# A two-layer hybrid trunk in float32: layer 0's shift and scale computed ahead, the gate's third behind the context's attention

## The reference

```
mod_x = silu(c)     @ w_ada[l] + b_ada[l]       # 3072 columns: shift, scale, gate
mod_c = silu(c_ctx) @ w_ada[l] + b_ada[l]
shift, scale, gate = split(mod, 3)
h = rmsnorm(x, g_pre) * (1 + scale) + shift     # the same for the context
p = h @ w_in                                    # projections of attention, conv, retention, fourier
y = merge(window_attention, short_conv, bidirectional_retention, fourier)
x = x + gate * rmsnorm(y, g_post)
```

## Time and profile before

| | us |
|---|---|
| three runs | 2643.99 to 2648.36, median 2647.52 |
| profiled execution | 2651.15 |
| its span | 2649.1 |
| TensorE busy | 2506.8 (95%) |
| VectorE, ScalarE, GpSimd busy | 1145.0, 1110.8, 1217.4 |
| chain that ended last | TensorE 79%, issue 8%, GpSimd 6%, VectorE 5%, ScalarE 2% |
| load of one unit (256 KB, 512-byte rows), issue to landing | 2.9 |
| load of `r_table` (320 KB), issue to landing | 2.9 |
| load of one `w_ada` block (1536 KB) | 9.1 |

### The profile page before, as it was taken

One profiled execution on the slowest core, in us unless ns is written; L12 is line 12 of the kernel. 1 busy time (PEld: TensorE's weight loads), 2 busy tenths in 40 slices (PEclk: granted clock), 3 DMA queues, 4 the chain that ended last, 5 costly groups with the idle time before them and its releaser, 6 DMA issues.

```text
span 2649.1 us, 39623 instructions
## 1 busy us (share of the span) xinstructions
PE 2506.8 (95%) x12993; PEld 2099.8 (79%) x12993; DVE 1145.0 (43%) x1698; ACT 1110.8 (42%) x2319; POOL 1217.4 (46%) x992
## 2 busy tenths in 40 slices
PE   7888979999999999999999979999999999999997
PEld 1887877899888767787888867898888788888886
DVE  2443655388153433334243367483444433333332
ACT  2635543288221454434433343594214433343332
POOL 1566963223222368865555442122212555555553
PEclk9898989999999999999999989999999999999999
DMA  6345663100121155544433431001210333344333
GB/s 238 96 126 163 175 186 105 45 4 6 48 65 33 36 148 159 159 127 131 147 109 107 146 116 40 24 2 34 64 43 21 106 111 111 111 135 143 111 111 119
DMA packets 390040, 262.37 MB, mean 99 GB/s; under 512 B 16006, under 2 KB 361238, under 8 KB 388378
## 3 DMA queue, kind: packets, MB, share of 16 engines
q1 hardware_dynamic: 377248, 227.07, 29.0%
q10 hardware_dynamic: 12668, 33.67, 3.6%
HBM read 251.23 MB, written 9.45 MB: 98 GB/s over the span
## 4 chain that ended last, share of the span: by engine, by line
PE 79%; issue 8%; POOL 6%; DVE 5%; ACT 2%; DMA 0%; ACTq 0%; POOLq 0%; DVEq 0%; SPq 0%
PE ps L671 75%; POOL w_lo L572 5%; PE ps L830 2%; DVE r_prev L2012 1%; DVE softmax_stats L1905 1%; DVE x_post L2227 0%; DVE a_probT_lo L1646 0%; DMA w_ada<-in_w_ada 0%; ACT a_prob L1334 0%; PE ps L770 0%; DVE norm_tmp L1791 0%; DVE a_out_sum L1646 0%; PE ps L816 0%; DVE proj_raw L1646 0%; PE ps L703 0%
## 5 line engine op out<-in xcount | busy, mean ns | idle before, releaser
L572 POOL TENSOR_TENSOR w_lo<-w_raw,w_hi 128x512 fp32r<-128x512 f32 x818 | 1113.5, 1373 | 1101.4 <-ACT w_hi L1166 1094.1
L671 PE MATMUL ps<-hT_hi,w_hi 128*128 128x512 f32 (+1 forms) x2528 | 948.7, 375 | 47.5 <-POOL w_lo L572 29.6
L671 PE MATMUL ps<-hT_lo,w_hi 128*128 128x512 f32 (+1 forms) x2528 | 934.8, 370 | 0.0
L671 PE MATMUL ps<-hT_hi,w_lo 128*128 128x512 f32 (+1 forms) x2528 | 934.5, 370 | 0.0
L1166 ACT ACTIVATE w_hi<-w_raw 128x512 fp32r<-128x512 f32 x818 | 507.5, 629 | 1006.9 <-PE ps L671 855.6
L671 PEld LDWEIGHTS ps<-hT_hi,w_hi 128*128 128x128 f32 x2528 | 484.4, 192 | 143.2 <-POOL w_lo L572 30.0
L671 PEld LDWEIGHTS ps<-hT_hi,w_lo 128*128 128x128 f32 x2528 | 484.3, 192 | 79.2
L671 PEld LDWEIGHTS ps<-hT_lo,w_hi 128*128 128x128 f32 x2528 | 484.9, 192 | 75.6
L1646 DVE TENSOR_TENSOR merge_tmp<-merge_tmp,ps 128x512 f32<-128x512 f32 (+1 forms) x160 | 101.6, 635 | 674.0 <-PE ps L671 411.4
L1646 DVE TENSOR_TENSOR merge_tmp<-merge_tmp 128x512 f32<-128x512 f32 (+1 forms) x120 | 170.8, 1423 | 4.1
L671 PE MATMUL ps<-yT_hi,w_hi 128*128 128x512 f32 (+1 forms) x400 | 148.3, 371 | 10.6 <-POOL w_lo L572 5.4
(11 more groups left out here) (260 smaller groups left out, 2800.0 us busy)
## 6 DMA issues: line engine op xcount, KB each, us to landing
w_raw<-in_w_in SPq DMA_DIRECT2D x512, 256.0 KB, 2.9
w_raw<-in_w_o_rest SPq DMA_DIRECT2D x120, 256.0 KB, 2.8
w_raw<-in_w_out SPq DMA_DIRECT2D x80, 256.0 KB, 2.6
w_ada<-in_w_ada SPq DMA_DIRECT2D x8, 1536.0 KB, 9.1
w_raw<-in_w_ada SPq DMA_DIRECT2D x48, 256.0 KB, 2.7
w_raw<-in_w_o_attn SPq DMA_DIRECT2D x40, 256.0 KB, 2.7
x_tile_first<-in_x ACTq DMA_DIRECT2D x8, 512.0 KB, 7.0
w_raw<-in_dft_x SPq DMA_DIRECT2D x16, 256.0 KB, 2.7
```

Of the source, the lines that this page charges most:

```text
L572: eng.tensor_tensor(w_lo[:, r, :], raw[:, r, :], w_hi[:, r, :].bitcast(F32), ALU.subtract).then_inc(sem["w_split"], tally.up("w_split"))
L671: return eng.matmul(dst, lhsT, rhs, start=start, stop=stop)
```

## The change

It has three parts. The context's tokens are loaded in `constants`, ahead of mask and `small`, and squared and scaled before the modulation. The modulation computes only shift and scale (2048 of 3072 columns): each block of `w_ada` is copied to a high part on ScalarE, its low part made on VectorE, and TensorE multiplies both with four columns, the high and low parts of the two silu vectors (64 fp32r products). The gate's third is loaded by ScalarE behind the context's attention, ahead of `r_table`, and multiplied in float32 in three groups between the projections; VectorE makes the gate row at that stage's end. The steps of `log_gamma` move to that stage too.

```diff
-        w_ada = at("w_ada", [P, KT, 3 * D], 0)
+        w_ada = at("w_ada", [P, KT, 2 * D], 0)
+        w_ada_lo = at("w_ada_lo", [P, KT, 2 * D], 0, F32R)
+        w_ada_hi = at("w_ada_hi", [P, 3, 2 * D], W + 2304, F32R)
+        w_ada_gate = [at("w_ada_gate", [P, KT - 1, D], Z + 3072), at("w_ada_gate_last", [P, D], W + 8448)]
...
             def ada(layer, k):
-                if k > 1:
-                    eng.wait_ge(ada_in[k - 2], 16)
-                eng.dma_start(w_ada[:, k, :], a["w_ada"][layer][k * P:(k + 1) * P, :]).then_inc(ada_in[k], 16)
+                if k > 2:
+                    eng.wait_ge(ada_in[k - 3], 16)
+                eng.dma_start(w_ada[:, k, :], a["w_ada"][layer][k * P:(k + 1) * P, 0:2 * D]).then_inc(ada_in[k], 16)
...
-            def modulation(l):
-                eng.wait_ge(sem["silu_c"], tally.take("silu_c"))
+            def modulation():
+
                 for k in range(KT):
-                    eng.wait_ge(ada_in[k], 16)
-                    for n in range(6):
-                        ins = mm(ps[0:2, n, :], sT[:, :, k], w_ada[:, k, n * 512:(n + 1) * 512], k == 0, k == KT - 1)
+                    eng.wait_ge(sem["ada_low"], tally.take("ada_low"))
+                    for n in range(4):
+                        c = slice(n * 512, (n + 1) * 512)
+                        mm(ps[0:4, n, :], s4[:, k, :], w_ada_hi[:, k % 3, c], k == 0, False)
+                        ins = mm(ps[0:4, n, :], s4[:, k, :], w_ada_lo[:, k, c], False, k == KT - 1)
...
+            def gate_sums(first, last):
+
+                eng.wait_ge(sem["gate_in"], tally.now("gate_in", 16 * 4))
+                for k in range(first, last):
+                    for n in range(2):
+                        c = slice(n * 512, (n + 1) * 512)
+                        w = w_ada_gate[0][:, k, c] if k < KT - 1 else w_ada_gate[1][:, c]
+                        ins = mm(ps[0:2, 6 + n, :], sT[:, :, k], w, k == 0, k == KT - 1)
+                        if k == KT - 1:
+                            ins.then_inc(sem["gate_sums"], tally.up("gate_sums"))
...
-                project(p, 8)
+                if p.opens:
+                    project(p, 4)
+                    gate_sums(0, 2)
+                    project(p, 2)
+                    gate_sums(2, 5)
+                    project(p, 2)
+                    gate_sums(5, KT)
+                else:
+                    project(p, 8)
...
                 eng.dma_start(ident[:, :], a["ident"]).then_inc(sem["const_in"], tally.up("const_in", 16))
+                tokens(passes[0], 0)
                 eng.dma_start(m_mask[:, :, :], a["mask"]).then_inc(sem["const_in"], tally.up("const_in", 16))
...
+                squares(p, 0)
+                for k in range(KT):
+                    eng.wait_ge(ada_in[k], 16)
+                    if k > 2:
+                        eng.wait_ge(sem["ada_used"], tally.take("ada_used"))
+                    act(w_ada_hi[:, k % 3, :], w_ada[:, k, :]).then_inc(sem["ada_high"], tally.up("ada_high"))
...
+            def gate_thirds(p):
+
+                l = p.layer
+                w = a["w_ada"][l][:, 2 * D:3 * D].rearrange("(k p) n -> p k n", p=P)
+                eng.dma_start(w_ada_gate[0][:, :, :], w[:, 0:KT - 1, :]).then_inc(sem["gate_in"], tally.up("gate_in", 16))
+                eng.dma_start(w_ada_gate[1][:, :], w[:, KT - 1, :]).then_inc(sem["gate_in"], tally.up("gate_in", 16))
...
                 stage_end(eng, tally, "act")
+                if p.opens:
+                    gate_thirds(p)
                 eng.dma_start(r_tab[:, :, :], a["ret"]).then_inc(sem["ret_in"], tally.up("ret_in", 16))
-                tile_range(p, B_U, B_B)
+                for t in range(B_U, B_B):
+                    tile_range(p, t, t + 1)
+                    if p.opens:
+                        log_gamma(t - B_U)
+                if p.opens:
+                    log_gamma(2)
                 decay_tables()
                 tile_range(p, B_B, R_Q)
+                if p.opens:
+                    gate_row(p)
                 stage_end(eng, tally, "act")
...
                 scaled(p, 0)
+                for k in range(KT):
+                    eng.wait_ge(sem["ada_high"], tally.take("ada_high"))
+                    tt(w_ada_lo[:, k, :], w_ada[:, k, :], w_ada_hi[:, k % 3, :].bitcast(F32), ALU.subtract).then_inc(
+                        sem["ada_low"], tally.up("ada_low"))
...
+            def gate_row():
+
+                eng.wait_ge(sem["gate_in"], 16 * 4)
+                for n in range(2):
+                    eng.wait_ge(sem["gate_sums"], tally.take("gate_sums"))
+                    c = slice(n * 512, (n + 1) * 512)
+                    tt(m_bias[0:2, c], ps[0:2, 6 + n, :], m_bias[0:2, c], ALU.add).then_inc(sem["dve_own"], tally.up("dve_own"))
+                eng.wait_ge(sem["dve_own"], tally.now("dve_own"))
+                tt(m_gate[0:2, :], m_bias[0:2, :], m_gate[0:2, :]).then_inc(sem["gate_made"], tally.up("gate_made"))
```

More of the change, by code:

```diff
@@ L233, in trunk @@
         x_tile = at("x_tile", [P, 4, D], W + 10240)
-        m_mask = at("mask_f32", [P, 2, P], W + 10240)
+        m_mask = at("mask_f32", [P, 2, P], W + 16384)
         n_sq = at("norm_square", [P, 4, 512], W + 14336)
@@ L1103, in _ @@
                 if p.ctx:
-                    modulation(p.layer)
+                    modulation()
                 elif p.kept:
@@ L1216, in modulation @@
-                tokens(p, 0)
-                squares(p, 0)
+                eng.dma_start(m_biasT[:, :], a["b_ada_cols"][l]).then_inc(sem["small_in"], tally.up("small_in", 16))
+                squares(p, 0)
[4 more added lines that the diff above has]
+                    act(w_ada_hi[:, k % 3, :], w_ada[:, k, :]).then_inc(sem["ada_high"], tally.up("ada_high"))
@@ L1218, in modulation, with gate_row @@
+            def gate_row(p):
                 eng.wait_ge(sem["gate_made"], tally.take("gate_made"))
-                eng.dma_start(gate_rows[l], m_gate[0:2, :]).then_inc(sem["gate_out"], tally.up("gate_out", 16))
-                eng.wait_ge(sem["gate_out"], tally.now("gate_out"))
+                eng.dma_start(gate_rows[p.layer], m_gate[0:2, :]).then_inc(sem["gate_out"], tally.up("gate_out", 16))
             def tokens(p, b):
@@ L1716, in modulation @@
                     tt(s4[:, :, 2 + s], sT[:, s, :], s4[:, :, s].bitcast(F32), ALU.subtract).then_inc(sem["dve_own"], tally.up("dve_own"))
-                eng.wait_ge(sem["small_in"], tally.take("small_in", 16 * 6))
-                for step in range(4):
-                    log_gamma(step)
+                eng.wait_ge(sem["dve_own"], tally.now("dve_own"))
                 scaled(p, 0)
-                for n in range(6):
-                    eng.wait_ge(sem["mod_rows"], tally.take("mod_rows"))
-                    c = slice(n * 512, (n + 1) * 512)
-                    tt(m_rows[0:2, c], ps[0:2, n, :], m_bias[0:2, c], ALU.add).then_inc(sem["mod_saved"], tally.up("mod_saved"))
@@ new lines, in modulation @@
+                for n in (1, 3):
+                    eng.wait_ge(sem["mod_rows"], n + 1)
+                    eng.tensor_copy(m_rows[0:4, n * 512:(n + 1) * 512], ps[0:4, n, :]).then_inc(sem["mod_saved"], tally.up("mod_saved"))
+                tally.skip("mod_rows", 4)
+                eng.wait_ge(sem["small_in"], tally.take("small_in", 16 * 5))
+                eng.wait_ge(sem["mod_cols"], tally.take("mod_cols"))
+                eng.tensor_copy(m_cols[:, :, :], ps[:, 6, 0:8 * KT].rearrange("p (k r) -> p k r", r=4)).then_inc(sem["dve_own"], tally.up("dve_own"))
@@ new lines, in modulation @@
+                eng.wait_ge(sem["dve_own"], tally.now("dve_own"))
+                for s in (1, 0):
+                    tt(m_sum[:, s, :], m_cols[:, :, s], m_cols[:, :, 2 + s], ALU.add).then_inc(sem["dve_own"], tally.up("dve_own"))
+                for s in (1, 0):
+                    eng.wait_ge(sem["dve_own"], tally.now("dve_own", -1))
+                    tt(m_sum[:, s, :], m_sum[:, s, :], m_biasT[:, 0:2 * KT], ALU.add).then_inc(sem["dve_own"], tally.up("dve_own"))
+                for s in (1, 0):
+                    eng.wait_ge(sem["dve_own"], tally.now("dve_own", s - 1 if s else -2))
+                    eng.tensor_copy(mod[:, s, 1, :], m_sum[:, s, 0:KT]).then_inc(sem["dve_own"], tally.up("dve_own"))
+                    eng.scalar_tensor_tensor(mod[:, s, 0, :], m_sum[:, s, KT:2 * KT], 1.0, gpre[:, :],
@@ L2253, in _ @@
                 stage_end(eng, tally, "dve")
+                if p.opens:
+                    for step in range(4):
+                        log_gamma(step)
                 convolution(p)
                 decay_tables()
+                if p.opens:
+                    gate_row()
                 stage_end(eng, tally, "dve")
```

34 lines of the change are left out of this document (17 added, 17 removed).

## The result

| | kernel before | changed kernel |
|---|---|---|
| median | 2643.36 us (10 runs) | 2660.24 us (10 runs) |
| ratio, 95% interval | | 1.0055 (1.0042 to 1.0067) |
| profiled execution, its span | 2651.15, 2649.1 | 2660.69, 2658.7 |
| granted clock over the span | 0.980 | 0.982 |
| TensorE busy | 2506.8 | 2493.2 |

The change makes the kernel slower by 0.55%, about 14.5 us; the medians are 16.9 apart. One of the ten executions of the changed kernel took 3945.25 us at a granted clock of 0.592; it is in the median and not in the ratio, and without it the medians are 16.4 apart. The sum of the prediction was +5.3, its forecast 2653 us, its range 2640 to 2663.

A forecast was written before the change was run, and what follows sets the result against it. It took 43.41 us of TensorE's float32 modulation products to bound the start, and a later stage to have only 5 us idle. -14.7 + 20.0 = +5.3 us, referred to the median 2647.52, gave 2653 us, range 2640 to 2663.

The forecast's parts named there:

- The constants' end: Start, ScalarE: the context's 1 MB ahead of mask and `small` delays it from 10.12 to 11.0 us, +0.9.
- Part 1: Modulation at the start: VectorE's subtractions are slowest, first modulated tile at 43.0 instead of 57.76 us, gain 14.7.
- R3: Rival, poorer start: slow subtractions or TensorE at 1.2 GHz (gain 5 to 10), or slower gate products; about 2660, chance 0.15.
- (a): Stage behind the context's attention: sixteen float32 gate products, 13.8 us on TensorE with 5 us idle, at least 8.8 added.
- (b): Same stage, ScalarE: four more load issues (1.5 us), two table loads and log steps (3.4 us); neither matters in the sum.
- (c): Same stage: `r_table` queues behind 4.2 MB of `w_ada`, lands at 141; ScalarE and all splits wait about 7 us.
- R1: Rival: no wait for `r_table`, loss 14.4 in the stage; net -1.5 to 0, about 2647 us, chance 0.22.
- (d): Same stage, TensorE-bound after the decay tables: next unit at about 179.8 against 157.35 us, loss 22.5.
- R2: Rival: gate products fill all idle time, only 8.8 us lost, start at its better end; net -8, about 2640, chance 0.18.
- (e): Behind the stage, 157 to 175 us: gate products fill the idle wait that had lowered TensorE's clock, 2.5 us back.
- The sum's anchor: Whole kernel: +5.3 us was referred to the median of 2647.52, 3.6 below the profiled execution's, giving 2653.
- the likeliest case: Whole kernel: the forecast itself, gain 14.7 and loss 20.0, total 2648 to 2659 us, chance 0.45.

The follow-up runs named there:

- e1: Changed kernel with the context's tokens loaded behind mask and `small` instead of ahead of them; 2659.13 us, ratio 1.0046 to the kernel before.
- e2: Changed kernel with `r_table` loaded ahead of the gate's 4.2 MB instead of behind; 2656.15 us, ratio 1.0040 to the kernel before.
- e8: e7 with the tokens' loads back behind the log steps and the last ten gate products behind TensorE's stage end; 2640.98 us, ratio 0.9988 to before.
- e7: e6 with gate's third loaded right behind the modulation, log steps at the start, gate products in two groups, gate row a stage later; 2643.19 us, ratio 0.9991.
- e5: Changed kernel with both load orders of e1 and e2; 2650.77 us, ratio 1.0022 to the kernel before.
- e6: Changed kernel with both orders of e5, and shift and scale as 32 float32 products without halves; 2650.53 us, ratio 1.0019 to before.

## Why the prediction was right or wrong

**The constants' end, +0.9 us (bounds 0 and 3): wrong, and the step that failed.** It measured +7.8 (10.12 to 17.89), and +7.0 in the second profile of the changed kernel (17.14). I priced the context's megabyte by its bytes (2.4 us at 430 GB/s) and took a part of it. What decides is when the last of 128 rows of a tiny load, queued behind that megabyte and beside `w_ada`, has landed. e1 put it ahead, which gave back all of it at the constants' end and 5.9 at the tile. The Trainium skill ("DMA: Bandwidth & Descriptors", Queues, rings and completion order) says that a DMA engine takes the descriptors of a ring in their order; e1, e2 and the changed kernel agree (5.5 against 13.8 us, 3.1 against 13.3). I had used that for `r_table` and not for `small`.

The order in the queue is only part of it. The tokens had landed at 11.92, `small` at 17.36. In the trace's transfers 93 of its 128 packets of 16 bytes have gone by the time of the tokens' last packet (10.99); the other 35 follow up to 16.58, among the 8 KB packets of `w_ada`, which begin at 7.61. In e1 all 128 are through by 7.24. And `mod_biasT`, 12 KB in ScalarE's queue, took 15.7 us in e8, where no large load stood ahead of it in that queue. So the megabyte seems to have cost most by pushing `small` in among `w_ada`'s packets in the other queue (it was also issued later, at 3.57 and not 2.47, with the first block of `w_ada` issued at 3.19). No run has the one without the other, so the shares are not shown. `mod_biasT` also speaks against the prediction's word that a table in a queue of its own would pass the 4 MB; that was not run.

**The rest of Part 1: right.** Copies 1908 ns (1.9 forecast), subtractions 2285 (2.28), TensorE at the full clock after 4 us, 32.5 us from the constants' end to the tile (32.0). "VectorE without gaps" was not so: the first products, at the lower clock, kept a buffer and so held it up for 1.4 us. The gain was 7.3 to 8.1 us, not 14.7: 6.9 of the 7.4 that are missing are the constants' end. R3 gave a gain of 5 to 10 with the total at 2660, and that is what came, but for another reason than the two it names: the subtractions were as forecast, and the clock held VectorE up by 1.4 us only. Its number came, its mechanism did not.

**(a) The products cost at least 8.8 us: right.** The unit that TensorE starts at 157.35 in the earlier trace rows starts at 154.00 in e7. Measured from the issue of `r_table` (124.94 and 112.69) that is 8.9 us later (9.9 against the second profile of before), with loads, log steps and gate row elsewhere.

**(b) The log steps:** the two table loads took 1.28 us each with the next operation right behind, as in the earlier trace rows; 3.4 us from 123.75 to 127.14. I called them hidden behind the wait for `r_table`, and they were: ScalarE had 5.33 us to spare behind them. In e2, without that wait, `r_xi` starts 9.9 us behind the stage's first issue instead of 15.3, so on ScalarE all of the 5.33 came back; 1.28 of it went into the wait for a weight load. The stage as a whole gained 3.3, and what took the rest of the difference is open, as is the price of the log steps alone.

**(c) `r_table` behind the gate's loads: right**, 5.33 us of waiting (7 forecast), landing at 132.4 (141 forecast). R1, no wait, is refuted. The forecast was late by its clock because the stage itself began 7.7 us earlier; from issue to landing it was 13.3 where I had 14.6.

**(d) The stage: right**, 22.25 us (22.5) for ScalarE's first split behind it; TensorE starts that unit at 171.97, 22.3 us later than before when both are measured from the stage's first issue. R2, 8.8 us only, is refuted for this kernel; e7 shows what it needs, loads that have landed and log steps elsewhere.

**(e) Given back, 2.5 us: right against one profile and not against the other.** The first split behind the stage comes 14.5 us later than before, but the chain piece behind it ends at 186.56 instead of 174.42, 12.1 later: 2.4 given back. In the second profile of before the same 120 matmuls took 16.16 us, not 17.07 (its chain):

```profile
156.66 16.16 PE ps L671 x120
```

Against it 1.5 us are given back (15.2 later at the split, 154.63 there, and 13.7 at the end of the piece). The slow clock that I counted as a cost of the kernel before was partly that one execution's.

**The sum's anchor.** With the measured terms, -7.5 at the start and +21 to +22.6 in the stage, the sum is +13.5 to +15; at split 80 it stands at +12.0 against the first profile of before and +16.4 against the second. The ratio says 14.5, the medians 16.9. So the trace explains the loss: a start that gained half of what was forecast, and a stage that lost what was forecast. The forecast was also 2653 and not 2649 because I referred it to a median of three runs, 2647.52; the median of ten is 2643.36, and the profiled execution of before was 7.8 above it.

**Range and luck.** 2660.24 lies outside the range of the likeliest case (2648 to 2659) and inside the whole one, where only R3 stood, with 0.15; "slower" had 0.40. Around its own anchor of 2647.52 the range was -7.5 to +15.5 us: the measured +14.5 is just inside it, and the +16.9 of the medians would not be. That the time fell into the range, with the start 7.4 us worse than forecast, is luck. Two sums of the rivals don't come out as written, either: R1's own terms give -2.3 to -1.3 and not -1.5 to 0, and R2 speaks of the start's better end (19 us) but adds up 14.7; with 19 it would be near 2635, below the range.

**Open.** Behind split 80 the profiles move against each other by some us where the program is the same (between splits 180 and 817 e1 and e5 lose 7, e6 nothing). The profiled execution of e5, 2658.49, was the slowest of its twelve and 7.7 above their median, and that of e1 the slowest of its six: the last column of the table is that of one execution. A single edit of 6 us at 250 us was therefore not found again in a median (e1), two together were (e5). Whether what e8 gains by split 80, 4.6 us more than before's second profile, is given back in the later passes or only not resolved, isn't settled.

## What to carry to other kernels

Price a load by who stands ahead of it in its queue and beside it, not by its bytes: where a stage's end waits for a small load, issue it first, and count it again for every large load that is moved ahead of it or comes to run beside it in another queue. Before moving work into a stage with idle time, check that its data and its helpers (here table loads on ScalarE and a product at the end) are not what the stage will wait for; the arithmetic itself was the smaller part (12 of 16 products, 6.3 of 21.0 us). And take two profiles of the kernel before, since a clock that is slow in one of them is not a term of the sum.

## What the runs showed of the hardware

- A load of 2 KB in 128 rows: 4.5 and 7.1 us in the two profiles of before, 5.0 to 5.9 with the 1 MB behind it in its queue (e1, e5 to e7), 10.5 to 13.8 with the 1 MB ahead. Another small load in ScalarE's queue (`mod_biasT`, 12 KB in 128 rows) took 12.2 us (changed kernel) to 17.0 (e1) while `w_ada` arrived in SyncE's, 15.7 with no large load ahead of it in its own (e8).
- `r_table`, 320 KB: 2.8 to 3.1 us alone or ahead, 13.1 to 13.7 behind 4.2 MB in the same queue.
- Weight loads of 256 KB in SyncE's queue: 2.8 to 3.4 us in that stage before, 9.3 to 10.2 beside 4.2 MB in ScalarE's queue (changed kernel), 8.7 to 10.1 (e2).
- Equal programs differ by 9.2 us at the end of two profiles (before), or by 1.0 (changed); between 157 and 200 us, where the difference begins, the granted clocks are 0.84 and 0.87 in the one and 0.91 and 1.00 in the other.
